# The three weight buffers of a ring, each 64 bytes further modulo 512

## What is computed

```python
# first block
proj = rms_norm(x) @ w_in                     # 1024 x 4256: heads of two attentions, 2048 gate logits
o_a = moba_attention(...) @ w_branch_a        # own causal block
o_b = mla_attention(...) @ w_branch_b         # after w_uq (384 x 768) and w_ukv (256 x 1024)
merged = gates_a * o_a + gates_b * o_b
x = x + rms_norm(merged @ w_out)
m = square(relu(rms_norm(x) @ w_up)) @ w_down # 1024 x 4096, 4096 x 1024
x = x + rms_norm(m)
# second block
proj = rms_norm(x) @ w_in_2                   # 1024 x 2560
x = x + concat(rms_norm(spatial_gating), rms_norm(dilated_attention)) @ w_out_2
xn = rms_norm(x)
q = xn @ w_query                              # 1024 x 2048: top-16 of 16384 experts in each of 8 heads
act = gelu(xn @ expert_u.T)                   # the kernel does all 16384 experts
x = x + (route_weights * act) @ expert_v      # the kernel does all 16384 experts
out = rms_norm(x)
```

## Time and profile before

| | |
|---|---|
| time, median of 2 runs | 1,266.61 us (1,266.40 to 1,266.82) |
| the profiled execution | 1,273.46 us |
| its span, first to last instruction | 1,271.7 us |
| instructions | 22,045 |
| PE busy | 1,261.8 us, 99% of the span |
| PEld, DVE, ACT busy | 1,149.9, 940.0 and 692.2 us |
| granted TensorE clock, mean | 0.999 |
| read from and written to HBM | 240.25 MB and 18.87 MB |

### The profile page before, as it was taken

The page is one execution under the profiler, slowest core; times in us unless marked ns, Lnnn a source line. Parts: engine busy times, 40 slices in busy tenths (PEclk is TensorE's granted clock), DMA queues, the critical chain, the costliest instruction groups (busy, mean ns, idle before and its releaser), DMA issues.

```text
span 1271.7 us, 22045 instructions
## 1 busy us (share of the span) xinstructions
PE 1261.8 (99%) x8615; PEld 1149.9 (90%) x8615; DVE 940.0 (74%) x1703; ACT 692.2 (54%) x1161; POOL 34.7 (3%) x29
## 2 busy tenths in 40 slices
PE   9999999999999999999999999999999999999998
PEld 8899989998878889999999999999988888888886
DVE  6776567774567867999989877878777667667666
ACT  6666457663455754444454455555644544554554
POOL 0000031000020010000000000000000000000000
PEclk9999999999999999999999999999999999999999
DMA  8543466666657345577777666666687677767763
GB/s 268 169 133 129 138 182 198 197 188 197 196 161 228 122 133 191 160 245 237 232 230 229 217 199 210 194 212 192 195 290 269 239 243 248 243 239 247 245 238 114
DMA packets 72807, 260.56 MB, mean 205 GB/s; under 512 B 8256, under 2 KB 9024, under 8 KB 72448
## 3 DMA queue, kind: packets, MB, share of 16 engines
q1 hardware_dynamic: 71232, 255.25, 62.0%
q0 software_dynamic: 1040, 3.34, 0.8%
q10 hardware_dynamic: 432, 0.56, 0.1%
HBM read 240.25 MB, written 18.87 MB: 204 GB/s over the span
## 4 chain that ended last, share of the span: by engine, by line
PE 95%; DVE 2%; ACT 1%; POOL 1%; issue 0%; DVEq 0%; ACTq 0%
PE ps L1086 27%; PE ps L484 16%; PE ps L492 14%; PE ps L493 14%; PE ps L494 14%; PE ps L1047 2%; PE ps L538 1%; PE ps L669 1%; PE ps L525 1%; POOL wlo L2394 1%; PE ps L531 1%; PE ps L1006 1%; PE ps L519 1%; ACT whi L1123 1%; PE ps L502 0%; PE ps L674 0%
## 5 line engine op out<-in xcount | busy, mean ns | idle before, releaser
L1628 DVE TENSOR_TENSOR wlo<-raw,whi 128x1024 fp32r<-128x1024 f32 (+2 forms) x410 | 498.0, 1216 | 267.1 <-ACT whi L1123 265.0
L1123 ACT ACTIVATE whi<-raw 128x1024 fp32r<-128x1024 f32 (+2 forms) x421 | 442.3, 1051 | 418.8 <-PE ps L1086 169.0
L492 PE MATMUL ps<-turned_x,whi 128*128 128x256 f32 x1504 | 425.4, 283 | 0.0
L493 PE MATMUL ps<-turned_x,whi 128*128 128x256 f32 x1504 | 418.7, 278 | 0.0
L494 PE MATMUL ps<-turned_x,wlo 128*128 128x256 f32 x1504 | 418.4, 278 | 0.0
L1086 PE MATMUL ps<-whi,turned_x 128*128 128x512 f32 x1024 | 315.3, 389 | 0.0
L492 PEld LDWEIGHTS ps<-turned_x,whi 128*128 128x128 f32 x1504 | 284.9, 189 | 0.0
L493 PEld LDWEIGHTS ps<-turned_x,whi 128*128 128x128 f32 x1504 | 282.9, 188 | 0.0
L494 PEld LDWEIGHTS ps<-turned_x,wlo 128*128 128x128 f32 x1504 | 282.4, 188 | 0.0
L1086 PEld LDWEIGHTS ps<-whi,turned_x 128*128 128x128 f32 x1024 | 192.2, 188 | 40.0 <-DVE wlo L1628 0.2
L1086 PE MATMUL ps<-wlo,turned_x 128*128 128x512 f32 x512 | 199.2, 389 | 0.0
(11 more groups left out here) (321 smaller groups left out, 1229.5 us busy)
## 6 DMA issues: line engine op xcount, KB each, us to landing
raw<-in_expert_u_dram SPq DMA_DIRECT2D x128, 512.0 KB, 4.1
raw<-in_expert_v_dram SPq DMA_DIRECT2D x128, 512.0 KB, 4.0
raw<-in_w_up_dram SPq DMA_DIRECT2D x32, 512.0 KB, 4.3
raw<-in_w_down_dram SPq DMA_DIRECT2D x32, 512.0 KB, 4.2
acts<-stage SPq DMA_DIRECT2D x32, 512.0 KB, 4.0
stage<-acts SPq DMA_DIRECT2D x30, 512.0 KB, 3.3
raw<-in_w_in_dram SPq DMA_DIRECT2D x20, 512.0 KB, 4.3
raw<-in_w_gate_dram SPq DMA_DIRECT2D x16, 512.0 KB, 3.4
```

Of the source, the lines that this page charges most:

```text
L492: e.matmul(dst, whi[:, h, sl], xh[:, k, :], start=k == 0, stop=False)
L493: e.matmul(dst, whi[:, h, sl], xl[:, k, :], start=False, stop=False)
L1123: e.activation(whi[:, u % NH, 0:n], raw[:, u % NR, 0:n], ACT.Copy).then_inc(*hi(u))
L1628: e.tensor_tensor(wlo[:, u % NH, 0:n], raw[:, u % NR, 0:n], whi[:, u % NH, 0:n].bitcast(F32), ALU.subtract).then_inc(*lo(u))
```

## The change

The ring becomes one tile `halves` of three buffers of 2,064 elements each, of which the first 1,024 are `whi`, the next 1,024 `wlo`, and 16 are unused; a buffer is 8,256 bytes, 16 times 512 and 64. `turned_x` grows by 16 elements, and `RH` and `RL` start 32 instead of 16 elements behind `TH` and `TL`. The tile of statistics, `st`, shrinks from 512 to 448 columns. The instructions, their order and their waits stay as they are.

```diff
-        whi = sb(ctx, "whi", [128, NH, 1024], F32R)
-        wlo = sb(ctx, "wlo", [128, NH, 1024], F32R)
+
+        halves = sb(ctx, "halves", [128, NH, 2064], F32R)
+        whi, wlo = halves[:, :, 0:1024], halves[:, :, 1024:2048]
         cst = sb(ctx, "cst", [128, CST_W])
         ppc = sb(ctx, "ppc", [128, PPC_W])
-        st = sb(ctx, "st", [128, 512])
-
-
-        turned_x = sb(ctx, "turned_x", [128, 4096 + 16], F32R)
-        TH, TL, RH, RL = (turned_x[:, a:a + 2048].rearrange("p (k n) -> p k n", n=256) for a in (0, 2048, 16, 2064))
+        st = sb(ctx, "st", [128, 448])
+
+
+        turned_x = sb(ctx, "turned_x", [128, 4096 + 32], F32R)
+        TH, TL, RH, RL = (turned_x[:, a:a + 2048].rearrange("p (k n) -> p k n", n=256) for a in (0, 2048, 32, 2080))
```

## The result

The changed kernel takes 1,298.09 us (1,297.96 to 1,298.21, 2 runs) against 1,266.61: 1.0248 times as long, interval 1.0204 to 1.0293. Predicted were 1,271, within 1,260 to 1,284. It is slower by 31.5 us, outside the range.

A forecast was written before the change was run, and what follows sets the result against it. The prediction took TensorE's matmul start distances to bound the kernel. Row form +4.5, column form 0 and the rest 0 gave +4.5 us on the median 1,266.6, so 1,271 us, range 1,260 to 1,284.

The forecast's parts named there:

- What bounds the kernel: Whole kernel: TensorE busy 99% of the span, so time is matmul count times start distance, plus a few waits.
- The column form: 4,512 matmuls streaming 256 columns, TH and TL held: leads move to -128, -192, -256; taken as 0, bounds -9.2 and +12 us.
- the row form: 2,208 matmuls with RH, MH, AH held, in expert_v, w_down, w_in_2, w_out_2: +4.5 us, bounds 0.9 and 10.8.
- the last rival: Column and row matmuls: each weight load pushed back as at w_uq's 120.0 ns; about 1,300 us, chance 0.04.
- The base: Whole kernel: +4.5 us added to the median 1,266.6, not to the profiled 1,273.46, giving 1,271.1 us.
- The term of +128: A third of the RH, MH, AH matmuls (736): no row shows this lead, priced like +64 at 1.8 us.
- the re-entry of a unit at lead 0: The third of RH, MH, AH matmuls keeping lead 0: 61 entries by 13 to 16 ns, 0.9 us.
- the sign that the prediction named: expert_v by unit: 226.7 ns in one buffer of three, about 229 in two; chain near 346 instead of 343.5 us.
- The rest: Matmuls streaming 512 columns with TH held (at most 0.7 us), w_uq and paired units (under 0.4), loads, splits, stores: taken as 0.
- Slow everywhere: Every column matmul costs 4.4 ns more, leads being farther from 0; 1,283 us against the median, chance 0.18.
- The weight load becomes the bound: Loads take 110 ns, close under 113.3; pushed back as in w_uq, +22 and +10.8 us, about 1,300; chance 0.04.
- Nothing moves: All stages: only streamed column count and entry set the pace, leads change nothing; 1,266.6 us (1,264.5 to 1,268), chance 0.17.

The follow-up runs named there:

- the constant kernel: Against the kernel before: whole ring 128 bytes on, TH at 0, so every unit has leads -256 (column form) and +128 (RH held); 1,304.30 us, 1.0302.
- the map: Separate kernel of matmuls alone, no block computed: 256 and 512 streamed columns at 32 leads in steps of 16 bytes; only paces given, no kernel time.
- the fine map: Matmuls alone again, 64 leads in steps of 4 bytes, then 16 entries each at leads -64 and -144; only paces given, no kernel time.
- the ring's step alone: Against the changed kernel: TH and TL put back to 64, giving buffer 0 the leads of the kernel before; 1,292.41 us, 1.0171 times before.

## Why the prediction was wrong

**What bounds the kernel: right.** Only start distances moved. Instructions, clock, VectorE and ScalarE are as before, and the sums of distances give 31.98 of 31.95 us.

**The column form: the step that failed.** The prediction took the nearest row, lead -64, for leads of -128 to -256, and priced them at 0 between bounds of -9.2 and +12 us. Measured against a profile with expert_u at the fast pace it is +21.10, and against a profiled execution like the one before (7.14 us more in this form) still +13.96, over the upper bound. Two things were wrong in it. The nearest row was no neighbour: -64 is one of two leads with 113.3 among 16, and -128, -192 and -256 showed no such pace from any entry. And the upper bound took 117.8, the slow pace at -64, for the worst, though w_uq's 120.0 at lead 0 stood in the rows and served as a price in the row form and in the last rival; at -256, the same lead modulo 256, the changed kernel shows 119.7 and the constant kernel 120.0. With 120.0 for all, the bound against a stream at 113.3 throughout would have been 4,512 by 6.7 = 30 us.

**The base.** The prediction saw that the 6.85 us between its profile and the median might be the slow stretch of expert_u. That was so. But it then added a column term made against a profile with expert_u at 117.8 to a median from executions that had it at 113.4; 7 of the 21 us were lost there.

**The row form: right in kind, half its size.** +9.46 us instead of +4.5, inside the bounds of 0.9 to 10.8. The term of +128 cost 6.2 ns a matmul where 2.4 was taken, +64 cost 3.6 (2.1 to 2.4 in a stretch that stays at it, by the map and the earlier trace rows), and the re-entry of a unit at lead 0 (230.63 - 226.67) by 12 = 47 ns where 13 to 16 was taken: the entry that the earlier trace rows shows came from another stage, and a unit that is entered from lead +128 is back only from its eleventh matmul. So the sign that the prediction named, one buffer of expert_v at 226.7, did not appear. An estimate of what the entries cost: 736 matmuls by the steady 2.4 ns and 736 by the 5.7 of the constant +128 are 6.0 us, which leaves about 3.5 of the 9.46.

**The rest.** Taken as 0; measured +0.6 with TH held, +0.6 in the branches, +0.2 otherwise.

**The rivals.** "Slow everywhere" was right in that the column form became slower in all three buffers, in expert_u by 4.4 to 6.4 ns against the fast pace where the rival had 4.4. Its reason is not shown, and its order by distance from 0 is wrong: -144 goes at 113.3 and -192 is faster than -128. "The weight load becomes the bound" came nearest in time, 1,300, but its mechanism isn't shown: at 64 streamed columns the distance is 110 ns before and after, and with 512 columns, which leave the load twice the time, the losses per matmul are as large. "Nothing moves" falls. Nor do the traces agree with the rule of the Trainium skill that the prediction weighed (TensorE: Matmul & The Clock Gate, Step-by-step: what each phase is for), as it read it: if loading the next weights took nothing from the running matmul, it should not matter where the held operand starts relative to the streamed one, and the fine map of matmuls alone has 113.3 to 123.3 ns for the same 256 columns. What inside the chip makes some leads better was not measured.

## What to carry to other kernels

Where TensorE is busy all the time in fp32r with a weight load per matmul, the start address of the streamed operand minus that of the held one, modulo 256 bytes, changes the distance by up to 6% with 256 streamed columns and 3% with 512 (in these kernels; in the fine map 9 and 6%), with no wait in the profile to point at it; read it from the start distance of each unit, not from busy time or mean durations. When a kernel is already at its fastest distances (here 113.3 and 226.7 ns), move the tiles around it in multiples of 256 bytes, or measure the new lead first, in the kernel itself. And where the profiled execution and the median differ, find the stretch that makes the difference before a sum is made against either.

## What was not expected of the hardware

- The best distances are 113.33 and 226.67 ns, at the granted clock of 2.4 GHz 272 and 544 cycles, 17/16 of the columns streamed. The Trainium skill (TensorE: Matmul & The Clock Gate, Back-to-back issue gap) has N/2.4 + 2.5 ns as the gap of a single matmul by itself, by which 256 and 512 columns would take an estimated 109.2 and 215.8; the streams here, with a weight load for each matmul, did not come below 113.3 and 226.6.
- One lead can hold two steady paces, chosen by the entry: -64 at 113.3 and 117.8. In the kernel before this splits the executions into two groups 7 us apart, with one interruption near the start of expert_u deciding for 67 units; with the ring's step alone it alternated from visit to visit in the first part of expert_u.
- The pace at a lead is periodic in 256 bytes, although a held slice is 512 bytes long and the ring's buffers more than 8,000 bytes apart.
